# Moving two groups of an output projection across a stage boundary, and filter products by one group

## The reference, cut to what matters

```python
h = (h - mu) * lax.rsqrt(var + EPS)                 # four heads, 512 values each
y = (h * norm_g + skip * xc) * jax.nn.sigmoid(o_pre)
return y @ out_w                                    # (512 x 2048) @ (2048 x 1024)
```

```python
z = jnp.sin(fr * (feat @ w1 + b1)); z = jnp.sin(fr * (z @ w2 + b2)); z = z @ w3
filt = z * jnp.exp(-tau[:, None] * decay[None, :])
return filt * lax.rsqrt(jnp.sum(filt * filt, axis=0, keepdims=True) + EPS)
```

## Time and profile before

| what | value |
|---|---|
| median of 3 runs | 2229.91 us (2228.94 to 2230.53) |
| the profiled execution, its own time | 2230.2 us |
| its span from first to last instruction | 2228.4 us |
| mean granted TensorE clock | 0.969 |
| TensorE busy | 2003.1 us, 90% of the span |
| DMA during the expert stages | 420 to 423 GB/s |

### The profile page before, as it was taken

The page is one execution under the profiler, slowest core; times in us unless marked ns, Lnnn a source line. Parts: engine busy times, 40 slices in busy tenths (PEclk is TensorE's granted clock), DMA queues, the critical chain, the costliest instruction groups (busy, mean ns, idle before and its releaser), DMA issues. The chain is left out here.

```text
span 2228.4 us, 20934 instructions
## 1 busy us (share of the span) xinstructions
PE 2003.1 (90%) x7680; PEld 899.1 (40%) x7680; DVE 790.4 (35%) x1593; ACT 374.8 (17%) x794; POOL 236.9 (11%) x523
## 2 busy tenths in 40 slices
PE   5999999999989959998888879999996999888883
PEld 2555444455443434442323324444454444333331
DVE  3777321245333752221111134463735221111123
ACT  2111213223202221111111112110102111111011
POOL 1000000000000012222222210000000222222221
PEclk9999999999999979999999999999996999999997
DMA  9798523131103489999999981121252999999995
GB/s 366 295 369 335 176 104 104 71 106 60 57 0 116 178 346 422 421 422 421 422 422 423 420 310 56 61 90 38 94 246 86 419 420 422 422 423 421 423 421 219
DMA packets 121181, 591.93 MB, mean 266 GB/s; under 512 B 25704, under 2 KB 43872, under 8 KB 80489
## 3 DMA queue, kind: packets, MB, share of 16 engines
q1 hardware_dynamic: 94494, 548.03, 61.1%
q10 hardware_dynamic: 14412, 25.59, 3.2%
q0 software_dynamic: 12160, 16.83, 2.1%
HBM read 571.13 MB, written 42.31 MB: 275 GB/s over the span
## 5 line engine op out<-in xcount | busy, mean ns | idle before, releaser
L566 PE MATMUL bank<-w,xT 128*64 128x512 f32 x1920 | 433.7, 598 | 47.4 <-DMA w<-in_moe_w 39.4
L586 PE MATMUL bank<-w,hT 128*64 128x512 f32 x1168 | 275.4, 614 | 47.3 <-DMA w<-in_moe_w 40.7
L566 PEld LDWEIGHTS bank<-w,xT 128*64 128x64 f32 x1920 | 153.9, 138 | 313.3 <-issue 262.4
L758 DVE COPY hT<-bank 128x256 f32<-128x256 f32 x73 | 30.9, 424 | 517.4 <-PE bank L574 517.4
L1163 PE MATMUL bank<-uhi,wnh 128*128 128x512 f32 x384 | 168.4, 593 | 0.9 <-ACT uhi L912 0.9
L586 PEld LDWEIGHTS bank<-w,hT 128*64 128x64 f32 x1168 | 88.7, 140 | 183.4 <-issue 137.2
L517 ACT ACTIVATE oh<-bank 128x256 f32<-128x256 f32 x73 | 28.0, 384 | 784.7 <-PE bank L566 784.7
L1559 PE MATMUL bank<-uT,wo 128*128 128x512 f32 x256 | 134.2, 606 | 3.2 <-DMA wo<-in_m_in_w 3.2
L763 DVE TENSOR_TENSOR ohs<-bank,g2h 128x512 f32<-128x512 f32 x73 | 50.5, 692 | 231.2 <-PE bank L586 231.2
L1163 PEld LDWEIGHTS bank<-uhi,wnh 128*128 128x128 f32 x384 | 71.8, 190 | 86.9 <-issue 85.8
L566 PE MATMUL bank<-w13x,xT 128*64 128x512 f32 x416 | 94.4, 593 | 8.0 <-DMA w13x<-in_moe_w 8.0
(11 more groups left out here) (441 smaller groups left out, 2175.2 us busy)
## 6 DMA issues: line engine op xcount, KB each, us to landing
w<-in_moe_w SPq DMA_DIRECT2D x177, 2048.0 KB, 35.0
adab<-in_ada_w SPq DMA_DIRECT2D x24, 2048.0 KB, 11.7
w13x<-in_moe_w SPq DMA_DIRECT2D x18, 2048.0 KB, 34.1
wnh<-in_h_in_w SPq DMA_DIRECT2D x12, 1024.0 KB, 5.2
wo<-in_m_in_w SPq DMA_DIRECT2D x4, 2048.0 KB, 17.8
wo<-in_m_in_w ACTq DMA_DIRECT2D x4, 2048.0 KB, 20.1
ow<-in_m_out_w SPq DMA_DIRECT2D x8, 1024.0 KB, 7.7
d_xm<-xmb ACTq DMA_DIRECT2D x16, 385.5 KB, 6.2
```

The source lines that it names most:

```text
L566: ins = t_.matmul(b[n * C:(n + 1) * C, :].rearrange("c (g f) -> c g f", g=2), xT[:, k, half * C:(half + 1) * C], w13s[i][:, k, n], start=( ...
L586: ins = t_.matmul(b_y[m * C:(m + 1) * C, :], hT[:, k, half * C:(half + 1) * C], w2[:, u, kk, m * 512:(m + 1) * 512], start=(kk == 0), stop ...
```

## The change

Two groups of half 0, head 0, token tiles 2 and 3 are issued in the head stage, behind the last transposes. The projection stage leaves them out. The numbers g of the groups stay, so the first filter product comes after group 4, the second after group 6, and the eight pairs after the groups 8 to 15.

```diff
+        BEFORE = 2
+        ORDER4 = (2, 3, 0, 1)
...
                 project_ahead(2)
                 back(HEADS - 1)
+                pe.wait_ge(s_ow[0], 16)
+                for t in ORDER4[:BEFORE]:
+                    for i in range(FT):
+                        if NUM["h", HEADS - 1, i] % 4 == t:
+                            pe.wait_ge(*freed[NUM["h", HEADS - 1, i]])
+                    for f in range(FT):
+                        t_.matmul(bank[t][:], yT[:, f, t * P:(t + 1) * P], ow[:, 1, out_part(0, 1).start + f, :], start=(f == 0), stop=False, skip_group_check=True)
...
-            FIRST = 7
+            FIRST = 8
...
-            ORDER4 = (2, 3, 0, 1)
...
                 for g, (i, t) in enumerate(groups):
-                    project(0, i, t)
-                    if g == 3:
+                    if g >= BEFORE:
+                        project(0, i, t)
+                    if g == 4:
                         pe.wait_ge(s_fld, 160)
                         t_.matmul(bank[4][0:HFH, :], fw1[:], ft[0:HEMB, :], start=True, stop=True).then_inc(s_zps, 1)
-                    if g == 5:
+                    if g == 6:
```

## The result

The changed kernel took 2236.28 us in the median (21 runs, 2230.53 to 2243.64) against 2231.78 us for the kernel before (21 runs, 2228.47 to 2236.79). The ratio is 1.0022, with a 95% interval of 1.0015 to 1.0029: 3.3 to 6.5 us slower, and above the forecast range of 2228.5 to 2235.0. The kernel before, at 2231.8 in these runs, lies 1.9 us above the three runs that the prediction had. The profiled execution of the changed kernel took 2233.42 us (span 2231.6), 3.2 more than the one of before.

What follows compares the result with a forecast made beforehand. TensorE's own sequence was taken to bound the projection stage's second half, so the sums move the end equally: +5.0 - 3.5 - 2.3 + 0 = -0.8, then +2.3, gives +1.5 on 2230.2: 2231.7 us, range 2228.5 to 2235.0.

Steps and rivals of the forecast that it cites:

- The opening, +5.0: Head stage's end: moved groups wait for bank 2 and end last, so the next stage opens 5.0 us later.
- The clock at the opening: Projection stage's opening: the 5.74 us gap becomes two short ones, the clock stays up, 2.3 us won.
- a rival at 0.15 and 2233.9 us: Head stage: the clock falls there too, transposes not counting as busy, costing some 2.2 us; chance 0.15.
- One group less, -3.5: Projection stage: one group less lies ahead of each filter product and pair, so the last pair comes 3.5 us earlier.
- The clock behind the sums, +2.3: Behind the sums: a new 5.3 us TensorE gap makes the clock fall, 2.3 us lost, bounds 0 and 2.9.
- The loads, 0: Projection stage: head 1's `ow` and the filter constants, needed earlier after the opening, still arrive in time, costing nothing.
- the rival of an early opening: Stage boundary: the barrier waits only for the moved matmuls' issue, so the stage opens at 670.76; 2230.3 us, chance 0.05.
- The weights late: Projection stage: `ow` for head 1 lands late, up to 5.2 us of wait plus 2.3 of clock; 2239.2 us, chance 0.05.
- the forecast sum: Whole kernel: opening, one group, both clock terms and loads together make it 1.5 us slower, at 2231.7 us.

Runs made afterwards that it cites:

- before, two traces: The kernel before, and the same kernel timed again without any edit under another name as a control; the control's ratio was 1.0002 (0.9993 to 1.0011).
- changed, two traces: The changed kernel against the kernel before, and again without any edit; ratios 1.0022 (1.0015 to 1.0029) and 1.0018 (1.0008 to 1.0028).
- groups alone: Changed kernel with its two moved groups, but the filter products put back at their old places; ratio to the kernel before 0.9997 (0.9988 to 1.0005).
- shift alone: Kernel before with only the filter products one group later and no group moved; ratio to the kernel before 1.0027 (1.0017 to 1.0037).
- sums' wait filled: Changed kernel plus four matmuls with discarded result in the wait before the sums; ratio to the kernel before 1.0015 (1.0007 to 1.0024).
- head gap filled: Changed kernel plus two discarded matmuls between the last transposes and the moved groups; ratio to the kernel before 1.0011 (1.0002 to 1.0020).
- both filled: Changed kernel plus two discarded matmuls ahead of the moved groups and four before the sums; ratio to the kernel before 0.9995 (0.9986 to 1.0004).
- early banks: Changed kernel, but the two moved groups are those of tiles 0 and 1, whose banks come free first; ratio to the kernel before 0.9996 (0.9988 to 1.0005).
- early banks, pairs back: Groups of tiles 0 and 1 moved, first products after groups 4 and 6, pairs back at groups 7 to 14; ratio to before 0.9990 (0.9980 to 0.9999).
- one group: Only tile 0's group moved into the head stage, filter products where they were before; 2227.98 us, ratio to the kernel before 0.9981 (0.9972 to 0.9989).
- five matmuls: Tile 0's group plus the first matmul of tile 1's group moved into the head stage; ratio to the kernel before 0.9984 (0.9974 to 0.9994).

## Why the prediction was wrong

The table has, from each trace's timeline, the time from the first of the last transposes to the opening, from there to the sums, and from the sums to the next filter matmuls (the products that spread the norms, 757.37 us in the first trace of before); then their sum against the mean of the two traces of before (93.9), and the measured ratio in us with its interval.

| kernel | opening | to the sums | behind them | sum against before | measured |
|---|---|---|---|---|---|
| before, two traces | 7.65, 7.65 | 71.68, 70.91 | 14.93, 14.93 | 0 | 0.4 (-1.6 to 2.5) |
| changed, two traces | 14.46, 14.47 | 65.92, 65.91 | 16.63, 17.99 | +3.1, +4.5 | 4.9 (3.3 to 6.5), 4.0 (1.8 to 6.2) |
| groups alone | 14.46 | 65.55 | 14.93 | +1.1 | -0.7 (-2.7 to 1.1) |
| shift alone | 7.65 | 75.06 | 17.15 | +6.0 | 6.0 (3.8 to 8.3) |
| sums' wait filled | 12.76 | 65.92 | 14.93 | -0.3 | 3.3 (1.6 to 5.4) |
| head gap filled | 12.70 | 65.92 | 17.42 | +2.2 | 2.5 (0.4 to 4.5) |
| both filled | 12.70 | 65.92 | 14.92 | -0.3 | -1.1 (-3.1 to 0.9) |
| early banks | 10.12 | 65.92 | 16.83 | -1.0 | -0.9 (-2.7 to 1.1) |
| early banks, pairs back | 10.13 | 63.33 | 14.92 | -5.5 | -2.2 (-4.5 to -0.2) |
| one group | 7.65 | 67.61 | 14.93 | -3.7 | -4.2 (-6.2 to -2.5) |
| five matmuls | 7.65 | 65.06 | 14.93 | -6.2 | -3.6 (-5.8 to -1.3) |

*The opening, +5.0.* The order of events was right: bank 2 ends the wait, VectorE's work hides only the first part, TensorE is the last to finish the stage, and the boundary costs 1.35 us behind TensorE too. With the clock up it is 12.70 - 7.65 = 5.05 us. But in both traces of the changed kernel it was 6.8.

*The clock at the opening, the step that failed.* The prediction took it that in the head stage's gap "the clock now stays up". Of the five traces with a gap of 2.3 to 2.4 us between the last transposes and the opening, four have the fall (8.80 us three times, 12.23 for 24 passes once), one has not. The term should have held a loss of 1.7 to 1.8 us ahead of the opening beside the 2.3 won behind it. The fall was carried as a rival at 0.15 and 2233.9 us; the profiled execution's 2233.42 is near that, which is luck, since the median of 21 is 2236.28. My evidence was one row: the gap of 2.33 us with a clock of 1.00 behind it. One gap that cost nothing doesn't show that gaps of its length are safe. The first trace had a second gap of this kind that I did not use, and it would have misled me too; the same gap in another kernel's trace has the fall (first line the kernel before, second the early banks):

```profile
1686.43 1.95 PE L228 MATMUL bank<-rw,zbci 128*128 128x36 f32 x16 [2.27 <-DVE zbci L1049]
1683.31 2.40 PE L228 MATMUL bank<-rw,zbci 128*128 128x36 f32 x16 [2.27 <-DVE zbci L1049]
```

This gap of 2.27 us, in the Hyena layer, stands in all 13 traces of this document. The granted clock in the 5 us behind it is 1.00 in four of them, the first traces of the kernel before and of the changed one among these, and 0.63 to 0.76 in nine, the second traces of both among those. The rival's reason, that transposes weigh less, is not needed: a gap with 512-column matmuls on both sides had the fall too. Whether transposes make it likelier is not tested. The opening itself was won as forecast: 24 passes in 10.54 us behind it.

*One group less, -3.5.* Right. From the opening to the sums it is 65.92 us, against 71.68 and 70.91, and the 5.8 or 5.0 us are 3.5 and the clock's 2.3 or 1.5. The 3.5 are two groups less (7.0) and 3.6 us more of waiting before the sums. The second group came back as waiting, as forecast: 5.31 us of idle time, and in the kernel with the shift alone 3.6 us of it with nothing to pay for it.

*The clock behind the sums, +2.3.* Right, as the mechanism and on the average: 1.7 and 3.1 in the changed kernel's two traces, 2.2, 2.5 and 1.9 in three others with the same gap.

*The loads, 0.* Right for the changed kernel, where no DMA ends a wait of TensorE. The spare time was as thin as computed: one group earlier, the constants were 1.30 us late.

*The boundary's barrier:* the opening came 1.35 us behind the moved matmuls' end in every trace with two of the groups in the head stage, so the rival of an early opening is out. *The weights late* did not occur.

*The base.* The forecast's 2231.7 us stood on one execution of 2230.2 us, 1.6 below the median of the 21 runs of before. Of the 4.6 us between 2231.7 and 2236.28, 1.6 are this base, 1.8 the clock in the head stage, and the rest is open. The prediction also took 4.5 us for what a measurement can't tell from no change; 21 runs on each side gave the difference to within 1.6 us.

With the head-stage fall the forecast sum becomes +1.5 + 1.8 = +3.3 us, at the edge of the first interval and inside the second. The rest, 1.6 us by the first comparison and 0.7 by the second, is not settled. Three measured times lie beside their single traces by 2.6 to 3.6 us (sums' wait filled, pairs back, five matmuls), which the three columns don't explain. A candidate is seen in the traces but not tested: the end of the projection stage, from the spreading matmuls to the expert stage's first VectorE instruction, takes 35.2 us in the first trace of before and 39.0 in the second, and 39 to 40 in the second of the changed kernel and in two of those three (all but the pairs back). A second such place lies behind the gap of 2.27 us: from there to the expert stage's first matmul it is 22.8 to 23.0 us in the four traces that kept the clock for 5 us and 26.2 to 27.4 in the nine others. Since such falls also come in the kernel before, a single trace can be off by several microseconds; whether they come more often in one kernel than in another is not tested.

## What to carry to other kernels

Work put into an idle stretch ahead of a barrier pays only for the part under the engine that ends last; here one group of 3.5 us fitted and two did not, and the buffers to choose are those that come free first. Count each place where the new order leaves the matmul engine idle, and price it twice, as idle time and as the slower clock behind it; moving the last product of a chain behind the last covering work turned 1.7 us of waiting into 5.3 and then cost 1.7 to 3.1 more. One row in which a short gap kept the clock is an instance and no bound: the sum needs both cases, and a second trace of the same kernel is a cheap way to see whether a gap behaves alike twice.

## What the runs showed of the hardware that I had not expected

A gap of TensorE of 2.3 to 2.4 us at the stage boundary was followed by a fall of the granted clock from 2.4 to 1.2 GHz in four of five traces. The Hyena layer's gap of 2.27 us had it in nine of 13. Of the expert stages' short gaps, the one of 2.33 us in the earlier trace rows did not have it, and of 16 of 1.9 to 2.1 us three had it. Behind long gaps it came each time: the 13 traces hold 71 gaps of 3.2 to 5.7 us that began at full clock, and in the 5 us behind each the clock averages 0.73 or less. So at about 2 us of idle time the same gap of the same program can have the fall in one execution and not in the next, as the two traces of the kernel before show (1.00 and 0.76 behind the 2.27 us).

The clock also falls with TensorE busy throughout. In the second trace of the kernel before the end of the projection stage is such a place; timeline and stretch:

```profile
781.40 3.66 PE L228 MATMUL bank<-rw,front 128*128 128x36 f32 x32
784.89 1.72 PE L222 MATMUL bank<-ident,hl 128*128 128x128 f32 x8
786.40 3.47 PE L234 MATMUL bank<-rwS,onesmat 128*128 128x36 f32 x16
789.68 3.61 PE L228 MATMUL bank<-rw,front 128*128 128x36 f32 x16
```
```profile
780.00:792.00 12.00, 12.00 (x77) 11.61 (x76) 4.54 (x16) 2.32 (x4) 0.00 (x0) 0.72 0.89 351
```

It follows 3.66 us of matmuls with only 36 columns; that these bring it about is not tested, and in most traces the same matmuls kept the clock. The last 16 passes then take 3.61 us where 16 of them took 1.95 in the first trace, whose stretch from 780 to 792 has a clock of 0.98. Nothing in the program differs between the two. The stretch from the spreading matmuls to the expert stage's first matmul is 47.9 to 48.5 us in four of the 13 traces and 44.1 in the nine others.
